# First layer of a two-layer decoder trunk: order of VectorE's work around the first scores, lambdas on GpSimd, shorter root chains, and a later broadcast of the FFN's row roots

## The chip, the cores and the metric

One core of one Trainium2 chip runs the whole program. The metric is device time in microseconds (us) of one execution, the median of 3 runs. The engines are TensorE (PE; PEld is its weight load), VectorE (DVE), ScalarE (ACT), GpSimd (POOL) and SyncE (SP), which issues the loads of the weights. Each engine executes its instructions in program order, and they meet at semaphores.

## The reference, cut to what matters

Two layers work on 256 tokens of width 1024 in float32. Each layer does the following.

```
h = rms_norm(x, norm_mix);  q, k, v = split(h @ w_in)          # 16 heads of 64: 4 diff, 6 dilated, 6 MoBA
q, k = rotary(rms_norm(q)), rotary(rms_norm(k))                # per head (diff: per half head of 32)
lam = exp(sum(lambda_q1 * lambda_k1)) - exp(sum(lambda_q2 * lambda_k2)) + lam_init
diff heads:  p = softmax(q1 k1) - lam * softmax(q2 k2);  o = rms_norm(p v) * (1 - lam_init)
x = x + concat(heads) @ w_out
x = x + memory_cross_attention(rms_norm(x), rms_norm(mem))     # 4 heads, 256 memory rows
x = x + swiglu(rms_norm(x))                                    # d_ff 2816
```

Every rms_norm needs a reciprocal square root of a mean of squares: for x, for the memory rows, and for each head of the queries and keys.

## The kernel before

**Split products.** The matmuls that touch weights are float32 products in three parts. A weight unit of 128 x 2048 values is loaded into `raw`. ACT rounds it to `whi` (`split_hi`), DVE makes the rest `wlo = raw - whi` (`split_lo`, line 927), and PE multiplies (hi, whi), (hi, wlo) and (lo, whi). There are three buffers of each (`RING = 3`). Unit u + 3 is loaded when both splits of unit u are done, and ACT's `split_hi` of unit u + 3 waits until PE has used unit u.

**The grid g.** The first part of each layer (q, k, v, the memory's keys and values, the output projection, and attention woven between them) is laid out by hand on a grid of steps g. At each g PE runs one piece of four matmuls of 512 columns (line 1572). Unit u is used by the six pieces from g = 6u on. Its `whi` is needed at 6u and its `wlo` one piece later. The other steps are placed by constants that name the g at which an engine's loop issues them. All engines walk the same g, each in its own loop, so these constants fix the order on each engine and not the time.

**Around the change, on DVE**, in the order of the loop body for one g: `mem_lo_part`, `mask_max` (masked scores and their maximum, line 1174), `combine` (line 1183 on), `qkT_out` (copies half of the transposed keys, even e, or queries, odd e, out of PSUM, lines 1155 and 1157), `reduce_squares` (line 1081), `lambdas`, `lambda_ends`, the memory rows' root at `MEM_ROOT_AT`, `split_lo`, then `norm_k` with `rope_k` or `norm_q` at `CHAIN_AT`. In the first 60 steps DVE therefore goes: g 7 split of unit 3; 10 `lambdas`; 13 squares 0, split 4; 14 `norm_k(0)`, `rope_k(0)`; 15 `lambda_ends`; 19 memory low part 0, split 5; 20 to 22 memory low parts 1 to 3; 25 squares 1, split 6; 26 `norm_q(0)`; 31 split 7; 32 `qkT_out(0)`; 37 squares 2, split 8; 40 memory root; 43 `qkT_out(1)`, split 9; 45 `mask_max` 0 and 1, `norm_k(1)`, `rope_k(1)`; 47 `mask_max` 2 and 3; 49 `combine` 0 and 1, squares 3, split 10; 53 `norm_q(1)`; 55 `mask_max` 4 and 5, split 11.

**On PE**: `transpose_qk(e)` (line 1665) at g = 32, 43, 58, 72. Even e are keys and wait for DVE's `rope_k`, odd e are queries and wait for GpSimd's `rope_q`. `score(d)` (line 1701) is at g = 45, 47, 55, 61 and waits for the maxima of the pair before (`nmax`), and for d = 0 for both copies of `qkT_out(1)`. The transposes of the probabilities `transpose_p` (line 1713) are at g = 54, 57 and wait for `combine`.

**On GpSimd**: `rope_q(half)` (lines 541 to 544). Its first four instructions wait for the squares of the queries, the other four for `norm_q`'s scaled queries. **On ACT**: the chunks of the projection out of PSUM (line 665), their squares (line 675), `split_hi` (line 605), the exponentials (line 697), and at g = `LAM_AT` + 3 the exponential of the lambdas (line 788), the first Exp of the program.

**Roots.** The heads' roots are computed on DVE by an integer first guess and three Newton steps of three small instructions, each waiting for the one before (`rsqrt`, `minus_rsqrt`, lines 936 to 955). The roots of x's rows and of the memory's rows are asked of GpSimd.

**FFN.** `gate_up(0, 0)` and `gate_up(0, 1)` open the FFN on PE (line 1978). Between them PE waits for `rs_diag` and broadcasts the roots of x's rows with a matmul with ones (line 2006); DVE copies the result to `rs_row` (line 1403). The roots are first used in `gate_step(0, 0)`.

Of the kernel before, what the change touches and what calls it, by code (L numbers as in the profile page):

```python
# [29 lines left out]
P = 128  # L30
F32 = mybir.dt.float32
F32R = mybir.dt.float32r
I32 = mybir.dt.int32
# [5 lines left out]
SEQ = 256  # L39
# [61 lines left out]
def trunk(nc, x, mem, w, gains, consts, out):  # L101
    with ExitStack() as ctx:
        def sb(name, shape, dt=F32):
            return ctx.enter_context(nc.sbuf_tensor(name, shape, dt))

        def signal(name, per_layer=1):
            return Signal(ctx.enter_context(nc.semaphore(name)), per_layer)
# [66 lines left out]
        h_root = sb("h_root", [P, 8])  # L174
        lam_dot = sb("lam_dot", [P, 2, DEPTH])
        lam_exp = sb("lam_exp", [P, 2, DEPTH])
        neg_lam = sb("neg_lam", [P, DEPTH])
# [43 lines left out]
        s_ones = signal("ones_set")  # L221
        s_lam = signal("lambda_ready")
        s_cs = signal("angles_ready")
        s_sin = signal("sines_ready")
# [230 lines left out]
        def _(pool):  # L455
# [53 lines left out]
            def norm_heads(y, gain, ready):  # L509
# [6 lines left out]
                    .then_inc(ready.sem, 1)  # L516

            pool.wait_ge(s_ones.sem, 1)
            for layer in range(DEPTH):
# [9 lines left out]
                ins.then_inc(s_tab.sem, 1)  # L529
                pool.wait_ge(s_tab.sem, s_tab.at(layer, 1))  # L530

                def rope_q(half):
# [378 lines left out]
        def _(dve):  # L911
            links = [0]

            def link(ins):

                links[0] += 1
                ins.then_inc(dve_chain.sem, 1)
                dve.wait_ge(dve_chain.sem, links[0])
# [12 lines left out]

            def rsqrt(n):


                v, h, y, t = (a[:, 0:n] for a in (nv, nh, ny, nt))
                dve.tensor_scalar(h, v, -0.5, None, ALU.mult)
                link(dve.tensor_scalar(y.bitcast(I32), v.bitcast(I32), -0.5, 1597463007.0, ALU.mult, ALU.add))
                for _ in range(3):
                    link(dve.tensor_tensor(t, y, h, ALU.mult))
                    link(dve.tensor_tensor(t, t, y, ALU.mult))  # L940
                    link(dve.scalar_tensor_tensor(y, t, 1.5, y, ALU.add, ALU.mult))

            def minus_rsqrt(n, out):


                v, h, y, t = (a[:, 0:n] for a in (nv, nh, ny, nt))
                dve.tensor_scalar(h, v, 0.5, None, ALU.mult)
                link(dve.tensor_scalar(y.bitcast(I32), v.bitcast(I32), -0.5, 1597463007.0, ALU.mult, ALU.add))
                for step in range(3):
                    link(dve.tensor_tensor(t, y, h, ALU.mult))  # L950
                    link(dve.tensor_tensor(t, t, y, ALU.mult))
                    if step < 2:
                        link(dve.scalar_tensor_tensor(y, t, -1.5, y, ALU.add, ALU.mult))
                    else:
                        link(dve.scalar_tensor_tensor(out, t.rearrange("p (t g) -> p t g", t=T), -1.5,
                                                      y.rearrange("p (t g) -> p t g", t=T), ALU.add, ALU.mult))

            def mean_eps(dst, sums, width):
                link(dve.tensor_scalar(dst, sums, 1.0 / width, EPS, ALU.mult, ALU.add))

# [59 lines left out]
            def lambdas():  # L1020

                dve.wait_ge(s_small.sem, 16)
                for i in range(2):
                    for l in range(DEPTH):
                        link(dve.tensor_tensor_reduce(nt[:, 0:32], lam_in[2 * i][:, l, :], lam_in[2 * i + 1][:, l, :],
                                                      1.0, 0.0, ALU.mult, ALU.add, lam_dot[:, i, l:l + 1]))
                for l in range(DEPTH):
                    ins = dve.tensor_scalar(g_sub[:, l, :], g_sub[:, l, :], 1.0 - lam_init(l), None, ALU.mult)

                    dve.tensor_tensor(g_km[:, l, :], g_km[:, l, :], g_qm[:, l, :], ALU.mult)  # L1030
                ins = dve.memset(nt[:, 0:32], 0.0)
                ins.then_inc(s_lam.sem, 1)

# [12 lines left out]
            for layer in range(DEPTH):  # L1046
# [37 lines left out]
                def norm_q(half):  # L1084

                    dve.wait_ge(reduced.sem, reduced.at(layer, 2 * half + 2))
                    n, first = ((12, 0), (8, 12))[half]
                    v = nv[:, 0:T * n].rearrange("p (t g) -> p t g", t=T)
                    sums = g32[:, 0]
                    if half == 0:  # L1090
                        dve.tensor_scalar(v[:, :, 0:8], sums[:, :, 0:8], 1.0, 32 * EPS, ALU.mult, ALU.add)
                        two = sums[:, :, 8:16].rearrange("p t (g w) -> p t g w", w=2)
                        link(dve.tensor_tensor(v[:, :, 8:12], two[:, :, :, 0], two[:, :, :, 1], ALU.add))
                        mean_eps(v[:, :, 8:12], v[:, :, 8:12], HD)
                    else:
                        dve.tensor_scalar(v[:, :, 0:2], sums[:, :, 0:2], 1.0 / HD, EPS, ALU.mult, ALU.add)
                        link(dve.tensor_scalar(v[:, :, 2:8], sums[:, :, 2:8], 1.0, HD * EPS, ALU.mult, ALU.add))
                    r = q_root[:, :, first:first + n]
                    minus_rsqrt(T * n, r)
                    a, b = ((8, 12), (0, 2))[half]  # L1100
                    z = heads_of_half(0, half)[:, :, ((256, 512), (0, 128))[half][0]:((256, 512), (0, 128))[half][1]]
                    z = z.rearrange("p t (g w) -> p t g w", w=HD)
                    for t in range(T):
                        ins = dve.scalar_tensor_tensor(z[:, t], z[:, t], -1.0,
                                                       r[:, t, a:b].unsqueeze(2).to_broadcast((P, b - a, HD)),
                                                       ALU.mult, ALU.mult)
                    ins.then_inc(scaled.sem, 1)

                def norm_k(half):
# [5 lines left out]
                    if half == 0:  # L1115
                        dve.tensor_scalar(v[:, :, 0:8], sums[:, :, 0:8], 1.0 / 32, EPS, ALU.mult, ALU.add)
# [5 lines left out]
                    rsqrt(T * n)  # L1122
                    r = ny[:, 0:T * n].rearrange("p (t g) -> p t g", t=T)
# [118 lines left out]
                for g in range(6, LAST + 1):  # L1242
# [9 lines left out]
                    for e in range(4):  # L1252
                        if g == QKT_AT[e]:
                            qkT_out(e)
                        if g == 12 * QK_CHUNKS[e] + 13:
                            reduce_squares(e)
# [226 lines left out]
        def _(pe):  # L1483
# [50 lines left out]
            for layer in range(DEPTH):  # L1534
# [114 lines left out]
                def transpose_qk(e):  # L1649
# [288 lines left out]
                output(1, (1,), (1, 2))  # L1938

                def gate_up(pair, b):  # L1940

# [22 lines left out]
                    for part, chunks in steps if b == 0 else ((part, range(KC)) for part in range(3)):  # L1964
# [69 lines left out]

CHAIN_AT = (14, 26, 45, 53)
QKT_AT = (32, 43, 58, 72)
# [61 lines left out]
def last_chunk(pair, b):  # L2098

    return isinstance(pair, int) and pair == PAIRS - 1 and b == 1  # L2100


# [90 lines left out]
```

## Time and profile before

| | us |
|---|---|
| median of 3 runs | 698.07 (697.97 to 698.45) |
| profiled execution | 698.69 |
| its span, first to last instruction | 696.9 |
| outside the span in that execution | 1.8 |
| PE busy in the span | 687.4 (99%) |
| DVE busy | 508.5 (73%) |
| ACT busy | 392.6 (56%) |
| GpSimd busy | 88.3 (13%) |
| granted TensorE clock, mean | 1.000 |

A busy time of PE is modelled from starts that overlap, so it hides waits below about 0.2 us. A line of the timeline reads: start, duration, engine, line, operation, output<-inputs, count, and in brackets the idle time of the engine before it with what ended it.

### The profile page before, as it was taken

The page shows a single profiled execution, that of the slowest core. Times are in us where ns is not written, and L with a number is a line of the kernel's source. Part 1 is how long each engine was busy: PE and PEld are TensorE (multiplying, and loading weights), DVE is VectorE, ACT ScalarE, POOL GpSimd, SP SyncE. Part 2 cuts the span into 40 slices and gives each one's busy share as a digit, 9 for nine tenths or more (in the row PEclk, how much of TensorE's full clock was granted, in tenths as well). Part 3 has the DMA queues.
Part 4 walks back from the last instruction along what each step waited for, and adds up shares of the span by engine and source line. Part 5 has one row for each costly group of instructions (what it writes and reads, how often), then busy time and mean ns, then how long its engine had stood idle before and what let it go on. Part 6 is the DMA issues. An engine that isn't in the chain of part 4 may idle for free.

```text
span 696.9 us, 10774 instructions
## 1 busy us (share of the span) xinstructions
PE 687.4 (99%) x3782; PEld 570.6 (82%) x3782; DVE 508.5 (73%) x1019; ACT 392.6 (56%) x637; POOL 88.3 (13%) x88
## 2 busy tenths in 40 slices
PE   8999999999999999999999999999999999999998
PEld 7876777788888888888888778778898888888886
DVE  5899977586766666666679898775777666666665
ACT  6965776477444444444566658764774444444442
POOL 5130111218000000000032210202530000000000
PEclk9999999999999999999999999999999999999999
DMA  9945341245576656666555635113365666666641
GB/s 325 327 130 178 123 162 57 85 122 156 160 222 187 181 181 181 181 181 184 186 174 199 228 118 179 64 61 112 100 213 141 196 200 197 199 194 194 186 120 61
DMA packets 121249, 115.66 MB, mean 166 GB/s; under 512 B 2688, under 2 KB 95104, under 8 KB 121216
## 3 DMA queue, kind: packets, MB, share of 16 engines
q1 hardware_dynamic: 120640, 114.31, 52.8%
q10 hardware_dynamic: 576, 0.93, 0.4%
q8 instruction: 19, 0.31, 0.2%
q14 instruction: 14, 0.11, 0.0%
HBM read 114.17 MB, written 1.05 MB: 165 GB/s over the span
## 4 chain that ended last, share of the span: by engine, by line
PE 81%; DVE 10%; ACT 3%; POOL 2%; issue 1%; DMA 1%; SPq 0%; ACTq 0%; POOLq 0%; DVEq 0%
PE ps L1951 21%; PE ps L1572 15%; PE ps L1956 11%; PE ps L1997 6%; PE ps L1998 6%; PE ps L1999 6%; DVE wlo L927 3%; PE ps L1643 3%; POOL wlo L497 2%; PE ps L1978 2%; PE ps L1701 2%; PE ps L1519 2%; PE ps L1713 2%; PE ps L1749 1%; DMA raw<-in_w_in 1%
## 5 line engine op out<-in xcount | busy, mean ns | idle before, releaser
L927 DVE TENSOR_TENSOR wlo<-raw,whi 128x2048 fp32r<-128x2048 f32 (+1 forms) x95 | 212.0, 2248 | 41.2 <-ACT whi L605 39.1
L605 ACT ACTIVATE whi<-raw 128x2048 fp32r<-128x2048 f32 (+1 forms) x102 | 188.7, 1876 | 14.7 <-PE ps L1572 8.1
L1951 PE MATMUL ps<-both,whi 128*128 128x512 f32 x640 | 159.2, 391 | 0.0
L1951 PEld LDWEIGHTS ps<-both,whi 128*128 128x128 f32 x640 | 117.7, 188 | 22.7
L1572 PE MATMUL ps<-whi,both 128*128 128x512 f32 x384 | 99.6, 396 | 1.3 <-ACT both L617 0.7
L1956 PEld LDWEIGHTS ps<-both,wlo 128*128 128x128 f32 x640 | 87.4, 191 | 6.2
L865 ACT ACTIVATE qkv<-ps 128x512 f32<-128x512 f32 x42 | 25.2, 599 | 114.3 <-PE ps L1956 113.6
L1956 PE MATMUL ps<-both,wlo 128*128 128x256 f32 x640 | 89.3, 283 | 0.0
L1572 PEld LDWEIGHTS ps<-whi,both 128*128 128x128 f32 x384 | 70.5, 188 | 17.2 <-issue 1.7
L1997 PE MATMUL ps<-whi,ahi 128*128 128x512 f32 x176 | 69.1, 393 | 0.0
L1998 PE MATMUL ps<-wlo,ahi 128*128 128x512 f32 x176 | 69.0, 392 | 0.0
L1999 PE MATMUL ps<-whi,alo 128*128 128x512 f32 x176 | 68.5, 389 | 0.0
L1414 DVE TENSOR_TENSOR qkv<-ps,qkv 128x512 f32<-128x512 f32 x42 | 28.9, 688 | 46.7 <-ACT qkv L865 46.6
L497 POOL TENSOR_TENSOR wlo<-raw,whi 128x2048 fp32r<-128x2048 f32 x7 | 32.0, 4606 | 183.6 <-DVE wlo L1468 179.5
L873 ACT ACTIVATE qkv<-qkv 128x256 f32<-128x256 f32 x44 | 18.4, 418 | 64.5 <-DVE qkv L1419 64.5
L1572 PE MATMUL ps<-wlo,both 128*128 128x512 f32 x192 | 53.4, 401 | 0.0
L697 ACT ACTIVATE sq<-sq,nm 128x128 f32<-128x128 f32 x80 | 35.5, 448 | 19.4 <-DVE nm L1174 19.4
L1572 PEld LDWEIGHTS ps<-wlo,both 128*128 128x128 f32 x192 | 34.6, 188 | 9.4 <-issue 2.7
L617 ACT ACTIVATE both<-ps,starter 128x128 fp32r<-128x128 f32 x96 | 26.6, 378 | 24.8 <-PE ps L1492 24.8
L1999 PEld LDWEIGHTS ps<-whi,alo 128*128 128x128 f32 x176 | 33.1, 188 | 7.2
L1997 PEld LDWEIGHTS ps<-whi,ahi 128*128 128x128 f32 x176 | 33.3, 189 | 5.7
L1998 PEld LDWEIGHTS ps<-wlo,ahi 128*128 128x128 f32 x176 | 33.3, 189 | 5.2
(214 smaller groups left out, 907.8 us busy)
## 6 DMA issues: line engine op xcount, KB each, us to landing
raw<-in_w_gate_up SPq DMA_DIRECT2D x88, 512.0 KB, 5.0
raw<-in_w_in SPq DMA_DIRECT2D x23, 1024.0 KB, 5.2
raw<-in_w_down SPq DMA_DIRECT2D x22, 1024.0 KB, 4.9
raw<-in_w_out SPq DMA_DIRECT2D x8, 1024.0 KB, 5.0
raw<-in_w_mkv SPq DMA_DIRECT2D x4, 1024.0 KB, 5.2
raw<-in_w_mq SPq DMA_DIRECT2D x4, 512.0 KB, 3.5
raw<-in_w_mo SPq DMA_DIRECT2D x2, 1024.0 KB, 4.7
xs<-in_x SPq DMA_DIRECT2D x4, 256.0 KB, 5.8
```

Of the source, the lines that this page charges most:

```text
L497: pool.tensor_tensor(wlo[s][:, 0:n], raw[s][:, 0:n], whi[s][:, 0:n].bitcast(F32), ALU.subtract)\
L605: ins = act.activation(whi[s][:, cols], raw[s][:, cols], ACT.Copy)
L617: ins = act.activation(thi[:, c, tok], ps[:, X_BANKS[b][q], k * P:(k + 1) * P], ACT.Copy, scale=gain)
L697: ins = act.activation(prob[n % 4][:, a:b], prob[n % 4][:, a:b], ACT.Exp, bias=nm[:, n, t:t + 1], scale=-1.0, accum_out=zs[:, n, t:t + 1])
L927: ins = dve.tensor_tensor(wlo[s][:, cols], raw[s][:, cols], hi, ALU.subtract)
L1414: dve.tensor_tensor(gu[b], gu_banks(b, 0), small_gu[b], ALU.add).then_inc(gu_done.sem, 1)
L1572: ins = pe.matmul(ps[:, acc, :], x_part[:, k0 + k, t * P:(t + 1) * P], w_part[s][:, 512 * k:512 * k + 512], start=first and k == 0 and par ...
L1951: pe.matmul(ps[:, bank, :], whi[s][:, a:a + P], both[:, :, k, :], start=(k == 0), stop=False)
L1956: ins = pe.matmul(ps[:, bank, 0:256], wlo[s][:, a:a + P], thi[:, k, :], start=False, stop=(k == KC - 1))
L1997: pe.matmul(acc, ahi[b][:, tok], whi[s][:, a:a + 512], start=first, stop=False)
L1998: pe.matmul(acc, ahi[b][:, tok], wlo[s][:, a:a + 512], start=False, stop=False)
L1999: ins = pe.matmul(acc, alo[b][:, tok], whi[s][:, a:a + 512], start=False, stop=last)
```

## The change

- `norm_k(1)` with `rope_k(1)` moves in the first layer from g = 45 to 50 on DVE (`CHAIN_AT[0][2]`).
- DVE's splits of units 8 and 9 move in the first layer from g = 37 and 43 to 45 and 49 (`LO_AT`).
- DVE's copy of the first half of the keys, `qkT_out(0)`, moves in the first layer from g = 32 to 27, ahead of the split of unit 7. PE's transposes stay at 32.
- The memory rows' root moves from g = 40 to 44.
- `lambdas` moves from g = 10 to 20, `lambda_ends` to 25 and ACT's exponential of them to 23. GpSimd makes the products and scales two gains ahead of its first `rope_q`; DVE keeps one reduction of 128 elements in place of the 13 instructions of before.
- `rsqrt` and `minus_rsqrt` become `cubic_root`: a first guess and two steps of four instructions each, in both layers. It has 9 instructions where 11 stood.
- PE's transposes of the first keys wait for two of the memory's four low parts, and those of the first queries for all four, where the former waited for all four.
- The broadcast of the row roots moves on PE from between the two `gate_up` of the first pair to after the first 16 matmuls of the second.

```diff
+            def lambda_products():
+                pool.wait_ge(s_small.sem, 16)
+                pairs = lam_products[:].rearrange("p (i l n) -> p i l n", i=2, l=DEPTH)
+                pool.tensor_tensor(pairs[:, 0], lam_in[0], lam_in[1], ALU.mult)
+                pool.tensor_tensor(pairs[:, 1], lam_in[2], lam_in[3], ALU.mult).then_inc(s_lam_products.sem, 1)
+                for l in range(DEPTH):
+                    pool.tensor_scalar(g_sub[:, l, :], g_sub[:, l, :], 1.0 - lam_init(l), None, ALU.mult)
+                link(pool.tensor_tensor(g_km, g_km, g_qm, ALU.mult))
...
-            def rsqrt(n):
...
+            def cubic_root(n, sign, out=None):
+                v, y, t, u = (a[:, 0:n] for a in (nv, ny, nt, nh))
+                link(dve.tensor_scalar(y.bitcast(I32), v.bitcast(I32), -0.5, 1597463007.0 - (sign < 0) * 2.0 ** 31,
+                                       ALU.mult, ALU.add))
+                for c in (1.0, ROOT_STEP):
+                    link(dve.tensor_tensor(t, y, v, ALU.mult))
                     link(dve.tensor_tensor(t, t, y, ALU.mult))
+                    link(dve.scalar_tensor_tensor(u, t, -10.0 / 3.0 * c, t, ALU.add, ALU.mult))
+                    if c == 1.0 or out is None:
+                        link(dve.scalar_tensor_tensor(y, u, 5.0 * c * c, y, ALU.add, ALU.mult))
...
             def lambdas():
-                dve.wait_ge(s_small.sem, 16)
...
+                dve.wait_ge(s_lam_products.sem, 1)
+                dve.tensor_reduce(lam_dot[:], lam_products[:].rearrange("p (i l n) -> p i l n", i=2, l=DEPTH), AX_X, ALU.add)\
+                   .then_inc(s_lam.sem, 1)
...
-                        if g == QKT_AT[e]:
+                        if g == QKT_DVE_AT[layer][e]:
                             qkT_out(e)
...
-                    if g % 6 == 1 and g // 6 + 2 < DVE_LO:
-                        split_lo(layer, g // 6 + 2)
+                    for u in range(3, DVE_LO):
+                        if g == LO_AT[layer][u - 3]:
+                            split_lo(layer, u)
                     for e in range(4):
-                        if g == CHAIN_AT[e]:
+                        if g == CHAIN_AT[layer][e]:
...
-                    if layer == e == 0:
-                        pe.wait_ge(m_lo.sem, 4)
+                    if layer == 0 and e < 2:
+                        pe.wait_ge(m_lo.sem, (2, 4)[e])
...
+                        if b and part == 0:
+                            rs_of_tokens()
...
-                pe.wait_ge(diag_ready.sem, diag_ready.at(layer, 1))
-                pe.matmul(ps[:, 4, 0:SEQ], ones[:], rs_diag, start=True, stop=True).then_inc(row_ps.sem, 1)
...
-CHAIN_AT = (14, 26, 45, 53)
+CHAIN_AT = ((14, 26, 50, 53), (14, 26, 45, 53))
+LO_AT = [[6 * (u - 2) + 1 for u in range(3, 18)] for _ in range(2)]
+LO_AT[0][8 - 3], LO_AT[0][9 - 3] = 45, 49
+QKT_DVE_AT = ((27, 43, 58, 72), (32, 43, 58, 72))
...
-LAM_AT = 10
-MEM_ROOT_AT = 40
+LAM_AT = 20
+MEM_ROOT_AT = 44
```

## Rows read from the trace of the kernel before

**Rows 1.** The page: granted TensorE clock in 40 slices of the span, in tenths.

```profile
PEclk9999999999999999999999999999999999999999
```

**Rows 2.** Timeline of PE in the first layer.

```profile
41.64 1.06 PE L1665 MATMUL ps<-starter,qkv 128*128 128x128 f32 x8 [0.70 <-DVE mlo L994]
...
52.57 1.04 PE L1665 MATMUL ps<-starter,qkv 128*128 128x128 f32 x8
...
56.23 0.93 PE L1701 MATMUL ps<-kT,qT 32*128 32x128 f32 x8 [0.80 <-DVE qT L1155]
...
67.59 0.55 PE L1713 MATMUL ps<-starter,sq 128*128 128x128 f32 x3 [0.41 <-DVE sq L1188]
...
73.06 1.03 PE L1665 MATMUL ps<-starter,qkv 128*128 128x128 f32 x8
...
77.13 0.93 PE L1701 MATMUL ps<-kT,qT 32*128 32x128 f32 x8 [0.30 <-DVE nm L1174]
```

**Rows 3.** Chain that ended last, second layer: start, us, what.

```profile
357.94 26.32 PE ps L1572 x116
```

**Rows 4.** Timeline of PE in the second layer.

```profile
407.14 1.07 PE L1572 MATMUL ps<-whi,both 128*128 128x512 f32 x4
408.26 0.55 PE L1713 MATMUL ps<-starter,sq 128*128 128x128 f32 x3
...
415.52 1.98 PE L1572 MATMUL ps<-whi,both 128*128 128x512 f32 x8
417.78 0.93 PE L1701 MATMUL ps<-kT,qT 32*128 32x128 f32 x8 [0.28 <-DVE nm L1174]
```

**Rows 5.** One group of DVE from 36.8 to 77: busy, mean ns, idle before.

```profile
L927 DVE TENSOR_TENSOR wlo<-raw,whi 128x2048 fp32r<-128x2048 f32 x7 | 16.1, 2304 | 0.4 <-ACT whi L605 0.4
```

**Rows 6.** Timeline of DVE in the first layer.

```profile
31.27 0.18 DVE L939 TENSOR_TENSOR nt<-ny,nh 128x24 f32<-128x24 f32 x1
...
33.23 0.69 DVE L1127 TENSOR_TENSOR qkv<-qkv,ny 128x512 f32<-128x512 f32 x1
...
36.37 0.15 DVE L1037 TENSOR_TENSOR neg_lam<-lam_exp 128x2 f32<-128x2 f32 x1
...
48.15 2.29 DVE L927 TENSOR_TENSOR wlo<-raw,whi 128x2048 fp32r<-128x2048 f32 x1
...
59.55 0.17 DVE L959 TENSOR_SCALAR nv<-g 128x16 f32<-128x16 f32 x1
...
64.99 0.34 DVE L1174 CUSTOM_DVE_ANT_0 sq<-ps,table,q_root 128x128 f32<-128x128 f32 x1
...
72.79 0.16 DVE L1096 TENSOR_SCALAR nv<-g 128x4 f32<-128x4 f32 x1
...
76.99 2.29 DVE L927 TENSOR_TENSOR wlo<-raw,whi 128x2048 fp32r<-128x2048 f32 x1
```

**Rows 7.** Timeline of ACT: second chunk's squares, and the Silu table in the FFN.

```profile
36.79 1.07 ACT L675 ACTIVATE sqc<-qkv 128x1024 f32<-128x1024 f32 x1
...
175.48 1.28 ACT L873 ACT_TABLE_LOAD   x1
178.85 0.42 ACT L873 ACTIVATE qkv<-qkv 128x256 f32<-128x256 f32 x1 [2.09 <-DVE qkv L1419]
```

**Rows 8.** Timeline of GpSimd: second half of the first `rope_q`.

```profile
48.38 2.38 POOL L541 TENSOR_TENSOR rope_pool<-qkv,tab 128x128 f32<-128x128 f32 x1 [7.26 <-DVE qkv L1104]
...
51.53 0.32 POOL L544 TENSOR_TENSOR qkv<-rope_pool 128x64 f32<-128x64 f32 x1
```

**Rows 9.** Timelines at the opening of the FFN: PE, then DVE, then PE.

```profile
173.59 1.12 PE L1978 MATMUL ps<-both,whi 128*128 128x256 f32 x8
174.92 0.70 PE L2006 MATMUL ps<-qkv,ones 128*128 128x256 f32 x2 [0.21 <-DVE qkv L1399]
...
180.09 0.42 DVE L1440 TENSOR_TENSOR alo<-qkv,ahi 128x256 fp32r<-128x256 f32 x1
...
181.21 0.40 PE L1997 MATMUL ps<-whi,ahi 128*128 128x512 f32 x1
```

More of the change, by code:

```diff
@@ L175, in trunk @@
         lam_dot = sb("lam_dot", [P, 2, DEPTH])
+        lam_products = sb("lam_products", [P, 2 * DEPTH * 32])
         lam_exp = sb("lam_exp", [P, 2, DEPTH])
@@ L222, in trunk @@
         s_lam = signal("lambda_ready")
+        s_lam_products = signal("lambda_products")
         s_cs = signal("angles_ready")
@@ L530, in _ @@
                 pool.wait_ge(s_tab.sem, s_tab.at(layer, 1))
+                if layer == 0:
+                    lambda_products()
                 def rope_q(half):
@@ L930, in split_lo @@
                 ins.then_inc(lo_done[s].sem, 1)
-            def rsqrt(n):
[L935 to L939, printed above, removed]
-                    link(dve.tensor_tensor(t, t, y, ALU.mult))
-                    link(dve.scalar_tensor_tensor(y, t, 1.5, y, ALU.add, ALU.mult))
@@ L943, in minus_rsqrt @@
[L943 to L953, printed above, removed]
+            def cubic_root(n, sign, out=None):
[4 more added lines that the diff above has]
+                    link(dve.tensor_tensor(t, y, v, ALU.mult))
+                    link(dve.tensor_tensor(t, t, y, ALU.mult))
+                    link(dve.scalar_tensor_tensor(u, t, -10.0 / 3.0 * c, t, ALU.add, ALU.mult))
+                    if c == 1.0 or out is None:
+                        link(dve.scalar_tensor_tensor(y, u, 5.0 * c * c, y, ALU.add, ALU.mult))
@@ L954, in minus_rsqrt @@
                     else:
-                        link(dve.scalar_tensor_tensor(out, t.rearrange("p (t g) -> p t g", t=T), -1.5,
+                        link(dve.scalar_tensor_tensor(out, u.rearrange("p (t g) -> p t g", t=T), 5.0 * c * c,
                                                       y.rearrange("p (t g) -> p t g", t=T), ALU.add, ALU.mult))
             def mean_eps(dst, sums, width):
-                link(dve.tensor_scalar(dst, sums, 1.0 / width, EPS, ALU.mult, ALU.add))
+                link(dve.tensor_scalar(dst, sums, ROOT_SCALE / width, ROOT_SCALE * EPS, ALU.mult, ALU.add))
@@ L1020, in lambdas @@
             def lambdas():
-                dve.wait_ge(s_small.sem, 16)
[L1023 to L1032, printed above, removed]
+                dve.wait_ge(s_lam_products.sem, 1)
+                dve.tensor_reduce(lam_dot[:], lam_products[:].rearrange("p (i l n) -> p i l n", i=2, l=DEPTH), AX_X, ALU.add)\
+                   .then_inc(s_lam.sem, 1)
             def lambda_ends():
@@ L1090, in norm_q @@
                     if half == 0:
-                        dve.tensor_scalar(v[:, :, 0:8], sums[:, :, 0:8], 1.0, 32 * EPS, ALU.mult, ALU.add)
+                        dve.tensor_scalar(v[:, :, 0:8], sums[:, :, 0:8], ROOT_SCALE, ROOT_SCALE * 32 * EPS, ALU.mult, ALU.add)
                         two = sums[:, :, 8:16].rearrange("p t (g w) -> p t g w", w=2)
@@ L1095, in norm_q @@
                     else:
-                        dve.tensor_scalar(v[:, :, 0:2], sums[:, :, 0:2], 1.0 / HD, EPS, ALU.mult, ALU.add)
-                        link(dve.tensor_scalar(v[:, :, 2:8], sums[:, :, 2:8], 1.0, HD * EPS, ALU.mult, ALU.add))
+                        dve.tensor_scalar(v[:, :, 0:2], sums[:, :, 0:2], ROOT_SCALE / HD, ROOT_SCALE * EPS, ALU.mult, ALU.add)
+                        link(dve.tensor_scalar(v[:, :, 2:8], sums[:, :, 2:8], ROOT_SCALE, ROOT_SCALE * HD * EPS, ALU.mult, ALU.add))
                     r = q_root[:, :, first:first + n]
-                    minus_rsqrt(T * n, r)
+                    cubic_root(T * n, -1, r)
                     a, b = ((8, 12), (0, 2))[half]
@@ L1115, in norm_k @@
                     if half == 0:
-                        dve.tensor_scalar(v[:, :, 0:8], sums[:, :, 0:8], 1.0 / 32, EPS, ALU.mult, ALU.add)
+                        dve.tensor_scalar(v[:, :, 0:8], sums[:, :, 0:8], ROOT_SCALE / 32, ROOT_SCALE * EPS, ALU.mult, ALU.add)
                         two = sums[:, :, 8:16].rearrange("p t (g w) -> p t g w", w=2)
@@ L1121, in norm_k @@
                         mean_eps(v, sums[:, :, 0:8], HD)
-                    rsqrt(T * n)
+                    cubic_root(T * n, 1)
                     r = ny[:, 0:T * n].rearrange("p (t g) -> p t g", t=T)
@@ L1938, in _, with rs_of_tokens @@
                 output(1, (1,), (1, 2))
+                def rs_of_tokens():
+                    pe.wait_ge(diag_ready.sem, diag_ready.at(layer, 1))
+                    pe.matmul(ps[:, 4, 0:SEQ], ones[:], rs_diag, start=True, stop=True).then_inc(row_ps.sem, 1)
                 def gate_up(pair, b):
@@ L2100, in last_chunk @@
     return isinstance(pair, int) and pair == PAIRS - 1 and b == 1
+ROOT_STEP = 64.0 / 9.0
+ROOT_SCALE = ROOT_STEP ** 6
 def lam_init(layer):
```

## The prediction, made blind

> **What bounds the kernel now.** I read the chain that ended last first. It is PE nearly throughout, except for the stretch from 18 to 77 us in the first layer, where links of DVE lie between PE's. The bracketed waits of PE's timeline say where: 0.70 at the first keys' transposes for the memory's low parts, 0.80 at the first scores for the copy of the queries, 0.41 at g = 54 for `combine`, 0.30 at g = 61 for the maxima [rows 2]. With about 0.5 between the first two scores, that is some 2.7 us. Apart from the opening of the span and one wait in each FFN [rows 9], PE shows nothing else of that size. The second layer runs the same grid, and PE keeps there a pace of 26.32 / 116 = 0.227 us a matmul, 0.91 a piece [rows 3]. Its small waits at g = 54 and 61 are seen by that pace: 407.14 + 0.92 = 408.06 against 408.26, and 415.52 + 1.92 = 417.44 against 417.78 [rows 4], 0.2 and 0.34. From g = 61 on, the layers lie the same distance apart at every piece (417.78 - 77.13 = 340.65 [rows 2, 4]). So what the change is worth in the first layer is the time at which the scores of g = 61 start, 77.13 now. All that follows is shifted by that.
>
> **The roots, both layers.** The nine linked instructions of a root take 33.23 - 31.27 = 1.96 us, 0.22 each [rows 6], with two more ahead of them, the first of which costs 0.1. Now there are one and eight, so a root is shorter by 0.22 + 0.09 = 0.3. Each layer has four. *Second layer:* the roots at g = 14 and 26 are hidden, for PE runs at pace there. The third is in front of `combine`, which comes 0.3 earlier and ends the 0.2 of g = 54. With the fourth the maxima of g = 61 come 0.6 earlier, more than 0.34, so PE goes on at pace there too. Gain 0.2 + 0.34 = 0.54, bounds 0.3 and 0.6. The queue behind DVE (its splits) comes earlier alike.
>
> **The broadcast in the FFN.** PE's eight matmuls from 173.59 would end their issue at about 174.55, and the broadcast starts at 174.92 [rows 9]: 0.36 lost. Behind 16 more matmuls (1.9 us) it starts at 176.5, well after the diagonal is ready. Its result comes at about 177.2, when DVE ends the split that it does in between, so `rs_row` isn't later. The cover is thin further on too: `alo` is done at 180.09 + 0.42 = 180.51, and PE then wants it at 181.21 - 0.36 = 180.85 [rows 9]. Gain 0.36 in each layer, 0.7 in all, bounds 0.3 and 0.8.
>
> **The first layer, by work alone.** DVE is the bound from the memory's low parts to g = 61, with 0.4 us of idle before the split of unit 10 [rows 5] and 0.1 before the second `combine`. Both orders hold the same work up to the maxima of g = 61, which ends at 76.99 [rows 6]. Off go four roots, 1.2, and these idle times, 0.5. On comes the reduction of the lambdas, 0.25 (bounds 0.15 and 0.4; small linked steps take 0.22, the squares of eight times the size more). The four products and the scalings that went to GpSimd save nothing: they lay in a gap in which DVE would have waited for the first squares. So DVE alone would be done at 75.5, and PE would gain 1.6. The wait of 0.70 for the memory's low parts goes, but PE then waits at the next transposes instead, as follows.
>
> **The first layer, by the new order.** I walked the four queues forward with the durations of the rows. New waits on DVE come in this order.
> - *Lambdas.* `rope_k(0)` ends at 36.37 - 0.3 = 36.1 [rows 6]. A low part, split 5, another low part and the reduction bring `lambda_ready` at 39.75. ACT comes to the exponential long before, at about 35, and is in order: behind it stand the chunk out of PSUM and the squares of the queries, which started at 36.79 [rows 7]. They now start at 40.6 and end at 41.7. DVE wants them at 40.9. Then `whi` of unit 6 follows, at 43.5, and split 6 waits for it a little more: 0.8 + 0.25 = 1.05. The table of Exp costs nothing extra, if it is loaded ahead of the wait as Silu's is (loaded at 175.48, used at 178.85 after a wait [rows 7]).
> - *First queries.* `norm_q(0)` ends at N = 48.85 (48.15 now [rows 6]). GpSimd's rotation then ran from 48.38 to 51.85, since its first instruction took 2.38 and ended only after DVE's split of 48.15 to 50.44 [rows 6, 8]. The last came 3.7 behind N. Now DVE's copy of the keys, 0.65, stands between N and split 7, so the blocking split ends 0.65 later, and the queries come at N + 4.35 = 53.2 at the worst. If the first instruction slips through in that gap, it is 52.75. PE, which would be there at 51.65 (52.57 now [rows 2], less 0.9 by the wait that went), stands until 52.8 to 53.25. The transposes' second half takes 1.1. DVE has the copy, split 7 and a reduction to do, 4.0, and waits 1.1 to 1.55 for it.
> - *First scores.* They start 2.75 after these transposes and are read 0.95 later, at 56.5 to 57.0. DVE is through with the copy and the memory root at 55.5 to 56.0, and waits 1.0. Splits 8 and 9, which filled this time before, are now behind.
> - *Second `combine`*, for the exponentials: 0.3.
>
> Sum of new waits 3.45 to 3.9, so the maxima of g = 61 come at 75.5 + 3.7 = 79.2, less 0.2 because the splits now run beside fewer instructions of GpSimd: 79.0. That is 2.0 later than 76.99, with bounds of 0.4 (GpSimd never blocked) and 2.4.
>
> **What PE sees.** It starts the first scores at about 55.8 and is ahead of now until g = 54 (some 65.9 against 67.59). It would reach the keys' transposes of g = 58 at 65.9 + 5.5 = 71.4. But `rope_k(1)` is no longer done at 64.99 [rows 6], eight us early. It now stands behind splits 8, 9 and 10, both `combine` and a reduction, and ends before `norm_q(1)` and the maxima, that is 4.2 - 0.3 = 3.9 before 79.0 [rows 6]: at 75.1. PE waits 3.7 us in one piece there, starts at 75.2 (73.06 now), needs 3.75 to g = 61 and starts those scores at 79.1. So the stall isn't removed but gathered in one place. `norm_k(1)` itself is 64.99 - 59.55 = 5.4 long [rows 6], one reason why it can't be late.
>
> **A rule beside it.** The row shows that a GpSimd instruction started in a split ends after it. The Trainium skill, GPSIMD Engine Reference, section 1 (Specifications), says that GpSimd shares its SBUF interfaces with VectorE where the latter has two SBUF inputs or a 2-port mode. By that rule the key copy, which reads PSUM, blocks nothing and the split does, so the better case of 52.75 would hold and the result would be 0.4 less than by the worst. The trace agrees as far as it goes.
>
> **Sum.** First layer +2.0, second layer -0.54, FFN -0.7: +0.75 of the profiled execution's 698.69 (span 696.9 and 1.8 outside it). I put the same difference on the median of the three runs, 698.07, which lies 0.6 below that execution: 698.8. Two tenths of a per cent are 1.4 us, about what can be told from no change.
>
> **The rivals.**
> - *No blocking.* GpSimd gets through before split 7; the queries are 1.6 earlier, the first layer ends at +0.4: 697.2. Against it: every rotation instruction that overlaps a split in the trace is long.
> - *DVE's bare work* (faster). The waits that I placed between engines don't arise or are filled, because the copies of keys and queries now come ahead of two low parts. Then g = 61 is at 75.5 and the first layer gains 1.6: 695.2. It decides where the new waits of DVE sum to less than about 1.5. For it: DVE is the only bound of the stretch now. Against it: the queue positions above.
> - *The clock falls* (slower). PE stands 3.7 us at g = 58, longer than anything in the trace of before, whose granted clock is full in all 40 slices [rows 1]. At the lower level (1.2 of 2.4 GHz) a piece would take 1.8 in place of 0.91. If it stays there for as long as the wait was, half of 3.7 is lost: 700.6. It decides at a wait of a length that no row shows. The Trainium skill, TensorE: Matmul & The Clock Gate, "Why this matters for your kernels", advises against gaps above about 3 us between bursts; by it this rival would hold.
> - *The table after the wait* (slower). If Exp's table is loaded only after `lambda_ready`, its 1.28 [rows 7] stands on ACT's way to the squares: 700.0. Against it: Silu's row.
>
> **How the numbers follow.** Forecast 0.52, no blocking 0.13, bare work 0.18, clock 0.11, table 0.06. Faster: bare work and a little of no blocking, 0.20. Slower: clock, table and the upper end of the forecast, 0.22. Same: 0.58. The range goes from halfway to the bare work, 696.2, to just past the table's time, 700.3; outside are the core of the bare work and most of the clock's case.
>
> **What would show it.** In the profile after: ACT idle before the exponential of the lambdas, some 3.5 to 4 us; DVE idle before its reduction of the queries' squares, before the queries' copy and before the first maxima; PE with one long wait at the transposes of g = 58 released by `rope_k`, and g = 61 at 79. In the second layer the scores of g = 61 0.5 us closer to the layer's start, and no wait at line 2006. I am wrong if PE's wait at g = 58 is under 2 us, if its clock row falls, or if `rope_k(1)` ends before 73.

## The result, and the profile after the change

The changed kernel takes 700.70 us (median of 6 runs, 700.40 to 701.76), the kernel before, run beside it, 698.19 (6 runs, 697.97 to 698.45). The ratio is 1.0038 [1.0028, 1.0048]: slower by 2.5 us, with the whole interval beyond 0.2%. I had forecast 698.8 and a range up to 700.3, so the time lies outside the range, on the side of the rival that I had given 0.11, the clock that falls.

The mean granted clock was 0.998 in four of the six runs (700.40 to 700.79 us) and 0.994 in the other two (701.48 and 701.76); before the change it was 1.000 in the profiled execution.

The profiled execution took 700.4 us (span 698.6), against 698.69 (696.9) before. These two differ by 1.7, not by the 2.5 of the medians: the profiled execution of before lies 0.5 above its kernel's median, and that of the changed kernel is the fastest of its six. The page shows no sign of the clock: its slices of 17 us still read 9 everywhere, as in [rows 1]. Only the mean over the span, which was 1.000, has moved:

```profile
core 0: 698.6 us, clock 0.998
```

PE's timeline in the first layer, which answers to [rows 2] (start, us, what, in brackets the wait before it):

```profile
52.54 1.09 PE L1662 MATMUL ps<-starter,qkv 128*128 128x128 f32 x8 [1.13 <-POOL qkv L558]
...
65.68 0.49 PE L1710 MATMUL ps<-starter,sq 128*128 128x128 f32 x3
...
70.08 1.17 PE L1569 MATMUL ps<-whi,both 128*128 128x512 f32 x4
75.20 1.97 PE L1662 MATMUL ps<-starter,qkv 128*128 128x128 f32 x8 [3.95 <-DVE qkv L1138]
76.82 1.82 PE L1569 MATMUL ps<-wlo,both 128*128 128x512 f32 x4
78.47 2.02 PE L1569 MATMUL ps<-whi,both 128*128 128x512 f32 x8
80.42 0.92 PE L1698 MATMUL ps<-kT,qT 32*128 32x128 f32 x8
```

Up to 75.20 this is the walk of the prediction: PE ahead of before until g = 54 (65.68; I said 65.9), then one wait for `rope_k(1)` of 3.95 (3.7) that ends at 75.20 (75.2). What comes next isn't. Eight transposes that took 1.03 before take 1.97, and four weight matmuls 1.82. The scores of g = 61 start at 80.42, not at 79.1.

A table of windows over the same stretch tells why (columns: window, its length, busy time of PE, PEld, DVE, ACT and POOL with instructions in parentheses, granted clock of PE, DMA share, GB/s):

```profile
70.00:75.00 5.00, 1.25 (x7) 0.73 (x5) 4.45 (x19) 0.00 (x0) 0.04 (x1) 0.98 0.95 359
75.00:76.00 1.00, 0.80 (x4) 0.80 (x5) 0.86 (x7) 0.00 (x0) 0.00 (x0) 0.50 0.06 25
...
77.00:78.00 1.00, 1.00 (x4) 0.81 (x4) 0.95 (x6) 0.00 (x0) 0.14 (x1) 0.50 0.00 0
78.00:79.00 1.00, 1.00 (x6) 0.77 (x5) 1.00 (x7) 0.58 (x3) 0.92 (x4) 0.88 0.00 0
79.00:80.00 1.00, 1.00 (x6) 0.83 (x5) 1.00 (x3) 1.00 (x4) 0.00 (x0) 1.00 0.02 8
```

At the end of PE's long wait the granted clock drops to 0.50, the lower of its two levels (1.2 of 2.4 GHz), and it is back after 78. In the trace it is low from 74.82 to 78.24, 3.4 us. PE had done nothing for some 3.6 us when it fell, and did work at half speed for the 3 us after 75.20.

DVE's timeline, which answers to [rows 6]:

```profile
41.36 1.22 DVE L1077 TENSOR_REDUCE g<-sqc 128x32 f32<-128x1024 f32 x1 [0.75 <-ACT sqc L689]
...
43.24 2.29 DVE L941 TENSOR_TENSOR wlo<-raw,whi 128x2048 fp32r<-128x2048 f32 x1 [0.22 <-ACT whi L619]
...
53.67 0.69 DVE L1151 COPY qT<-ps 128x512 f32<-128x512 f32 x1 [1.04 <-PE ps L1662]
...
56.38 0.35 DVE L1170 CUSTOM_DVE_ANT_0 sq<-ps,table,q_root 128x128 f32<-128x128 f32 x1 [0.93 <-PE ps L1698]
...
65.12 4.68 DVE L941 TENSOR_TENSOR wlo<-raw,whi 128x2048 fp32r<-128x2048 f32 x2
...
74.89 0.25 DVE L1138 TENSOR_TENSOR qkv<-rope_dve 128x96 f32<-128x96 f32 x1
...
78.98 2.29 DVE L941 TENSOR_TENSOR wlo<-raw,whi 128x2048 fp32r<-128x2048 f32 x1
```

The four new waits of DVE are there: 0.75 + 0.22 for the first queries' squares, 1.04 before the queries' copy, 0.93 before the first maxima. The splits of 65.12 (units 9 and 10) stand ahead of `norm_k(1)` and `rope_k(1)`, whose last instruction, at 74.89, is the one that PE waits for. The maxima of g = 61 end where the next split starts, at 78.98 (79.0 said, 76.99 before).

ACT waits in front of the exponential of the lambdas, with its table loaded ahead of the wait, and the queries' squares are behind it, 3.5 us later than in [rows 7]:

```profile
34.45 1.28 ACT L802 ACT_TABLE_LOAD   x1
39.45 0.20 ACT L802 ACTIVATE lam_exp<-lam_dot 128x4 f32<-128x4 f32 x1 [3.72 <-DVE lam_dot L1027]
39.56 0.67 ACT L679 ACTIVATE qkv<-ps,rs 128x512 f32<-128x512 f32 x1
40.27 1.06 ACT L689 ACTIVATE sqc<-qkv 128x1024 f32<-128x1024 f32 x1
```

On GpSimd, where [rows 8] show 2.38 for the first instruction of the rotation, that one now slips through and the second is the long one:

```profile
48.78 0.46 POOL L555 TENSOR_TENSOR rope_pool<-qkv,tab 128x128 f32<-128x128 f32 x1 [5.75 <-DVE qkv L1100]
49.20 2.60 POOL L556 TENSOR_TENSOR rope_pool<-qkv,tab 128x128 f32<-128x128 f32 x1
```

DVE's split 7 starts at 49.22. So this was the better of my two cases: PE's transposes start at 52.54, against the 52.8 to 53.25 that I had walked.

Then PE in the FFN and in the second layer, which answers to [rows 9] and [rows 4]:

```profile
176.86 3.04 PE L1980 MATMUL ps<-both,whi 128*128 128x256 f32 x24
179.74 0.59 PE L1940 MATMUL ps<-qkv,ones 128*128 128x256 f32 x2
179.98 2.26 PE L1980 MATMUL ps<-both,wlo 128*128 128x256 f32 x16
...
183.99 0.40 PE L2001 MATMUL ps<-whi,ahi 128*128 128x512 f32 x1
...
419.97 0.93 PE L1698 MATMUL ps<-kT,qT 32*128 32x128 f32 x8
```

The broadcast (179.74) has no wait, nor have the second layer's scores. By these anchors the span's +1.7 splits up as follows:

| Stretch (PE start to PE start) | before | after | difference | forecast |
|---|---|---|---|---|
| to the memory rows' first transposes | 27.01 | 26.69 | -0.3 | 0 |
| from there to the scores of g = 61, layer 1 | 50.12 | 53.73 | +3.6 | +2.0 |
| to the FFN's first down matmul | 104.08 | 103.57 | -0.5 | -0.36 |
| to the scores of g = 61, layer 2 | 236.57 | 235.98 | -0.6 | -0.54 |
| to the second FFN's first down matmul | 104.08 | 103.54 | -0.5 | -0.36 |

All terms but one are within about 0.3. The -0.3 of the first row is no gain that can be told: in the ten traces of this case those transposes start anywhere from 26.38 to 27.02. The first layer has 1.6 more than forecast. Its maxima end 2.0 later while the whole stretch began 0.3 earlier, so DVE's order costs 2.3; the other 1.3 is between `rope_k(1)` and g = 61, at the low clock.

### The profile page after: what moved, and what is told of

Read it like the earlier page. It is cut to its first block, busy times and chain, and to the rows that moved or that the text cites. A ratio compares the mean times of both kernels' runs of the same rounds, so it can differ in the third digit from the quotient of the medians.

```text
span 698.6 us, 10753 instructions
## 1 busy us (share of the span) xinstructions
PE 688.4 (99%) x3782; PEld 572.1 (82%) x3782; DVE 505.3 (72%) x991; ACT 392.2 (56%) x637; POOL 94.3 (14%) x93
## 3 DMA queue, kind: packets, MB, share of 16 engines
HBM read 114.17 MB, written 1.05 MB: 165 GB/s over the span
## 4 chain that ended last, share of the span: by engine, by line
PE 92%; DVE 5%; ACT 1%; DMA 1%; issue 1%; POOL 1%; SPq 0%; DVEq 0%; ACTq 0%; POOLq 0%
PE ps L1569 21%; PE ps L1953 21%; PE ps L1958 11%; PE ps L2001 6%; PE ps L2002 6%; PE ps L2003 6%; PE ps L1980 3%; PE ps L1640 3%; PE ps L1698 2%; PE ps L1516 2%; DVE wlo L941 2%; PE ps L1710 2%; PE ps L1885 2%; PE ps L1489 1%; PE ps L1746 1%; PE ps L1858 1%
```

## The experiments

Every kernel ran beside the kernel before on the same chip (one chip for e1 to e4, another for e5 to e8): beside e1 to e4 the kernel before had 698.24 in the median of 30 runs, beside e5 to e8 698.27 in 27, with a clock of 0.999 or 1.000. These two values of the mean are called the full clock below; 0.998 and less are called low. Three questions stood against each other: is the second half of the loss the clock; is it one long wait that lowers it; and does the loss that is left come from the queue of DVE, or from the parts (roots, lambdas, broadcast)?

| Kernel | median, us | runs | lowest to highest | ratio [95%] | PE's waits, 49 to 82 us |
|---|---|---|---|---|---|
| after | 700.70 | 6 | 700.40 to 701.76 | 1.0038 [1.0028, 1.0048] | 1.13, 3.95 |
| e1 | 700.88 | 7 | 699.07 to 702.03 | 1.0031 [1.0020, 1.0042] | 1.1, 1.69, 2.27 |
| e2 | 699.20 | 11 | 698.78 to 699.54 | 1.0013 [1.0004, 1.0022] | 1.1, filled + 1.23 |
| e3 | 699.54 | 11 | 698.77 to 700.53 | 1.0018 [1.0009, 1.0027] | 3.94 |
| e4 | 697.44 | 11 | 696.77 to 699.10 | 0.9991 [0.9982, 1.0000] | 0.91, 1.42, 0.48 |
| e5 | 698.39 | 11 | 697.84 to 700.48 | 1.0002 [0.9993, 1.0011] | 0.88, 1.42 |
| e6 | 697.33 | 11 | 695.42 to 698.90 | 0.9986 [0.9976, 0.9995] | 1.98 |
| e7 | 697.02 | 11 | 696.50 to 697.25 | 0.9980 [0.9971, 0.9989] | 0.5, 0.5 |
| e8 | 695.51 | 5 | 695.44 to 695.78 | 0.9960 [0.9947, 0.9974] | 1.22 |

### e2: the long wait filled

DVE's order is left as the change has it. PE is given matmuls of ones, into the bank of the transposes that follow, to do in its wait.

```diff
@@ PE, at every g @@
+                    if layer == 0 and g == QKT_AT[2]:
+                        warm_up(FILL, QKT_BANKS[2][0])
+FILL = 12
```

> The changed kernel with 12 more transposes-sized products of ones (24 matmuls of 128 columns, some 3.6 us at full clock) on PE right before the transposes of g = 58 in the first layer, into the bank that these overwrite. They add no work that the output needs. Clock theory: PE's idle time there falls from 3.95 to about 0.4 us, the clock stays 1.000, the eight transposes take 1.0 in place of 1.97 us, the scores of g = 61 start at 79.1, the time is 698.9 us. Rival (the loss stands in DVE's queue only): nothing changes, 700.5 us, or more by the added matmuls.

PE's timeline, and one window:

```profile
71.01 2.84 PE L1526 MATMUL ps<-ones 128*128 128x128 f32 x24
75.09 1.10 PE L1662 MATMUL ps<-starter,qkv 128*128 128x128 f32 x8 [1.23 <-DVE qkv L1138]
...
79.01 0.92 PE L1698 MATMUL ps<-kT,qT 32*128 32x128 f32 x8
```

```profile
75.00:76.00 1.00, 0.91 (x9) 0.92 (x9) 0.86 (x7) 0.00 (x0) 0.00 (x0) 1.00 0.12 47
```

The filling took 2.84 us and not the 3.6 that I expected, so 1.23 us of the wait stays empty. The keys come no sooner (75.09), but the clock stays at 1.00 in the window behind the wait, the transposes take 1.10, and g = 61 starts at 79.01, where I had put it. From the transposes to g = 61 it is 3.92 here and 5.22 in the changed kernel: 1.3 for the clock. The medians say 1.50 (700.70 - 699.20), in which the changed kernel's two runs at 0.994 have a part: its four at 0.998 have a median of 700.58, 1.38 above e2. What is left by the medians, +0.96 over before, stands against the prediction's +0.75; by the two profiled spans (697.3 and 696.9) it is +0.4. So the clock is about 1.5 of the 2.5, and the forecast without it lies between these two.

### e1: one split behind the keys

```diff
 LO_AT[0][8 - 3], LO_AT[0][9 - 3] = 45, 49
+LO_AT[0][10 - 3] = 51
```

> The changed kernel with one more constant: DVE's split of unit 10 in the first layer goes from g = 49 to 51, behind norm_k(1) and rope_k(1). DVE's work and its sum stay the same, so the maxima of g = 61 still end near 79.0. Clock theory (the long wait lets TensorE's clock fall, and that is what came on top of the forecast): the keys are ready 2.2 us earlier, PE's wait at the transposes of g = 58 is 1.7 us in place of 3.95, the granted clock stays 1.000, the scores of g = 61 start at 79.1 in place of 80.4, and the time is 698.9 us or less. Rival (DVE's late end alone, or a transposition that is slow for another reason, makes the loss): 700.5 us, as the changed kernel.

PE's timeline, and one window:

```profile
72.65 1.09 PE L1662 MATMUL ps<-starter,qkv 128*128 128x128 f32 x8 [1.69 <-DVE qkv L1138]
...
78.76 1.49 PE L1698 MATMUL ps<-kT,qT 32*128 32x128 f32 x8 [2.27 <-DVE nm L1170]
```

```profile
79.00:80.00 1.00, 1.00 (x8) 0.52 (x6) 1.00 (x1) 1.00 (x4) 0.00 (x0) 0.50 0.18 66
```

This was a miss, and the miss taught most. The keys were 2.5 earlier, and the maxima of g = 61 as late as in the changed kernel, both as I had said; what I had overlooked is that PE, which comes to g = 61 earlier, must then wait there for these maxima. The wait was split in two, 1.69 and 2.27, neither as long as the one of 3.95. Still the clock fell, at 78.97, and stayed low for 6.83 us, twice as long as after the single wait; the profiled run took 702.03. Of the seven runs, the two whose mean clock was 0.999 and 1.000 took 699.32 and 699.07, about e2's time; the other five (0.995 to 0.998) 700.68 to 702.03. At the full clock, then, keys that come 2.5 earlier gain nothing, since DVE's maxima set g = 61. A single long wait isn't what decides about the clock, and the time of a kernel depends on whether the clock falls in that very execution.

### e3: the lambdas' exponential late

```diff
-                    if layer == 0 and g == LAM_AT + 3:
+                    if layer == 0 and g == LAM_EXP_AT:
-                    if layer == 0 and g == LAM_AT + 5:
+                    if layer == 0 and g == LAM_ENDS_AT:
+LAM_EXP_AT, LAM_ENDS_AT = 31, 44
```

> The changed kernel with ACT's exponential of the lambdas at g = 31 in place of 23 and DVE's lambda_ends at g = 44 in place of 25. Theory of the queues: ACT no longer stands 3.7 us before the exponential, the squares of the queries come 1.6 us earlier, DVE loses its waits of 0.75 and 0.22 us before the squares' reduction and split 6, and the maxima of g = 61 end 1.0 to 1.2 us earlier. PE's wait at g = 58 stays 3.7 to 4 us long, because PE comes earlier too, and the clock still falls: 699.4 us. Rival (ACT's wait is hidden by other slack): 700.5 us.

ACT's timeline, then PE's:

```profile
35.58 1.06 ACT L689 ACTIVATE sqc<-qkv 128x1024 f32<-128x1024 f32 x1
...
42.28 0.20 ACT L802 ACTIVATE lam_exp<-lam_dot 128x4 f32<-128x4 f32 x1
```

```profile
74.08 1.14 PE L1662 MATMUL ps<-starter,qkv 128*128 128x128 f32 x8 [3.94 <-DVE qkv L1138]
...
79.45 0.92 PE L1698 MATMUL ps<-kT,qT 32*128 32x128 f32 x8
```

With the exponential at g = 31 the squares are back at 35.58, and everything of DVE comes about 1 us earlier, as expected. PE's wait keeps its length, for PE is earlier too, and so does the loss of clock (0.994 to 0.998 in the runs). The median, 699.54 against 699.4 expected, is 1.16 below the changed kernel: that is what ACT, blocked in order, costs.

### e4 and e5: the old order, with the new parts

e4 takes DVE's old positions back, and keeps the roots, GpSimd's lambdas and the moved broadcast. e5 takes the broadcast back too.

```diff
-CHAIN_AT = ((14, 26, 50, 53), (14, 26, 45, 53))
+CHAIN_AT = ((14, 26, 45, 53), (14, 26, 45, 53))
-LO_AT[0][8 - 3], LO_AT[0][9 - 3] = 45, 49
-QKT_DVE_AT = ((27, 43, 58, 72), (32, 43, 58, 72))
+QKT_DVE_AT = ((32, 43, 58, 72), (32, 43, 58, 72))
-MEM_ROOT_AT = 44
+MEM_ROOT_AT = 40
@@ only e5: PE, between the gate_ups of the FFN @@
-                        if b and part == 0:
-                            rs_of_tokens()
+                rs_of_tokens()
```

> The changed kernel with the first layer's order of DVE as before (norm_k(1) at 45, splits 8 and 9 at 37 and 43, the keys' copy at 32, memory root at 40). Left of the change: roots of 9 instructions, lambdas on GpSimd at g = 20, the two low-part waits, the late broadcast. Theory: the order alone makes the loss. PE has no wait above 1.5 us in the first layer, clock 1.000, scores of g = 61 at 77.1 as before (what the roots save there is lost again to ACT's wait for the lambdas), second layer -0.55, FFN -1.0: 696.6 us. Rival (the lambdas or the roots cost more than they save): 698 us or more.

> The changed kernel with the first layer's order of DVE as before, and the broadcast of the row roots back between the two gate_up of the first pair. Left: the roots, the lambdas on GpSimd, the low-part waits. Theory: the late broadcast is worth 0.5 us in each layer, as the two traces show, so this kernel takes 1.0 us more than the one with the old order alone (697.4): 698.4 us. Rival (what the broadcast gains is given back before the next layer): 697.4 us.

In e4 the keys of g = 58 are in time again, and PE waits elsewhere (timeline):

```profile
52.53 1.09 PE L1662 MATMUL ps<-starter,qkv 128*128 128x128 f32 x8 [0.91 <-POOL qkv L558]
...
56.89 0.92 PE L1698 MATMUL ps<-kT,qT 32*128 32x128 f32 x8 [1.42 <-DVE qT L1151]
...
77.19 0.92 PE L1698 MATMUL ps<-kT,qT 32*128 32x128 f32 x8
```

g = 61 starts at 77.19, as before the change (77.13): roots and lambdas together gain the first layer nothing. The roots alone gain it 1.1 (e7, below). In e4 ACT still stands 3.39 us before the exponential of the lambdas, and DVE behind it 0.75 and 0.23, which e7 has not, so the lambdas take back most of what the roots give. e4 is 3.26 faster than the changed kernel, so the moved positions of DVE, with the clock that they cost, are the whole loss. I had expected 696.6 and a full clock; it is 0.8 more, and the clock was low in six of the 11 runs. The five at the full clock have a median of 697.12, so 0.5 of the miss isn't the clock. e5 came as expected (698.39 against 698.4), and the broadcast's new place is worth 697.44 against 698.39: 0.95, or 0.48 a layer, which agrees with the 0.5 a layer of the table above. The runs at the full clock alone say the same: 697.12 against 698.08, five of each.

Both kernels lose clock in six of 11 runs. e5's profiled run (700.48) was one, and its windows and timeline show it after waits of only 0.88 and 1.42 us, with work in between:

```profile
55.00:59.00 4.00, 2.58 (x16) 1.68 (x15) 3.15 (x6) 0.69 (x1) 0.73 (x1) 1.00 0.78 256
60.00:65.00 5.00, 5.00 (x17) 3.21 (x16) 4.49 (x19) 2.28 (x9) 0.00 (x0) 0.50 0.57 210
```

```profile
60.56 1.65 PE L1698 MATMUL ps<-kT,qT 32*128 32x128 f32 x8
```

### e7: the roots alone

The kernel before, with `cubic_root` for both roots (and the scaling it needs) and nothing else.

```diff
-            def rsqrt(n):
-            def minus_rsqrt(n, out):
+            def cubic_root(n, sign, out=None):
...
-                    minus_rsqrt(T * n, r)
+                    cubic_root(T * n, -1, r)
-                    rsqrt(T * n)
+                    cubic_root(T * n, 1)
```

> The kernel before with the roots of two steps alone, in both layers. Theory: DVE is the only bound up to the scores of g = 61 in the first layer, so three of the four roots (0.3 us each) move them by 0.9 to 1.2 us, and the second layer gains 0.55 by its two small waits: 696.6 us. Rival (the stretch is bound by PE or by ACT as well): 0.55 us, 697.7.

PE's timeline:

```profile
76.04 0.92 PE L1691 MATMUL ps<-kT,qT 32*128 32x128 f32 x8
```

This part, alone, is a gain: 697.02, 1.25 less than before, with g = 61 at 76.04 (77.13 in [rows 2]) and the clock full in all 11 runs. I had expected 696.6, so it came 0.4 short, though well clear of the rival's 697.7. In the traces the terms are there: g = 61 is 1.09 earlier (0.2 of which lies ahead of the memory rows' first transposes, where the traces differ anyway), and the second layer 0.58 shorter. The old order in the first layer could use the shorter roots.

### e6 and e8: another order

Both move the lambdas' end as e3 does, leave the keys' copy at g = 32, and put `rope_k(1)` ahead of a split again; e8 differs from e6 by one number, the place of split 10.

```diff
-CHAIN_AT = ((14, 26, 50, 53), (14, 26, 45, 53))
+CHAIN_AT = ((14, 26, 49, 53), (14, 26, 45, 53))
-LO_AT[0][8 - 3], LO_AT[0][9 - 3] = 45, 49
+LO_AT[0][9 - 3], LO_AT[0][10 - 3] = 45, 51
-QKT_DVE_AT = ((27, 43, 58, 72), (32, 43, 58, 72))
+QKT_DVE_AT = ((32, 43, 58, 72), (32, 43, 58, 72))
+LAM_EXP_AT, LAM_ENDS_AT = 31, 44
@@ only e8 @@
-LO_AT[0][9 - 3], LO_AT[0][10 - 3] = 45, 51
+LO_AT[0][9 - 3], LO_AT[0][10 - 3] = 45, 55
```

> The changed kernel with another order in the first layer, found by the same walk along the queues: ACT's exponential of the lambdas at g = 31, lambda_ends at 44, the keys' copy at 32, split 8 at 37, split 9 at 45, norm_k(1) and rope_k(1) at 49, split 10 at 51. Theory: DVE always has a split in hand while GpSimd, PE and ACT work on the queries, the keys of g = 58 are ready before PE comes, no wait of PE in the first layer is above 0.5 us, the clock stays 1.000, the scores of g = 61 start at 75.5 (77.1 before), and with 1.6 from the second layer and the FFN the time is 695.4 us. Rival (the walk leaves out a wait that the old order hid): 697 us or more.

> The kernel e6 with split 10 of the first layer at g = 55, behind the maxima of g = 61. Theory: the scores of g = 61 could start at 73.6, but the piece of g = 61 needs split 10, which ends at 75.6, so a wait of 1.2 us moves from the scores to that piece, and the gain over e6 is 0.8 us at most: 694.8 us. Rival (DVE's whole work decides, wherever the split stands): as e6.

e6, PE's timeline and two windows:

```profile
75.66 0.92 PE L1698 MATMUL ps<-kT,qT 32*128 32x128 f32 x8 [1.98 <-DVE nm L1170]
...
77.67 3.44 PE L1569 MATMUL ps<-whi,both 128*128 128x512 f32 x8
```

```profile
77.00:78.00 1.00, 1.00 (x5) 0.82 (x4) 1.00 (x2) 1.00 (x5) 0.00 (x0) 0.69 0.00 0
78.00:79.00 1.00, 1.00 (x4) 0.71 (x4) 0.93 (x4) 1.00 (x4) 0.00 (x0) 0.50 0.17 14
```

The scores of g = 61 start at 75.66, where I had walked them, but PE waits 1.98 there, which I had not seen, and the clock falls afterwards: its mean of 0.69 between 77 and 78 puts the fall at about 77.4, 1.7 us after PE had gone back to work. Eight matmuls take 3.44 in place of 1.98. The clock was low in 9 of 11 runs; the two with a clock of 0.999 took 695.42 and 695.66, the time that I had forecast for all of them.

In e8 split 10 gives way to the maxima (PE's timeline):

```profile
73.61 0.92 PE L1698 MATMUL ps<-kT,qT 32*128 32x128 f32 x8
75.76 1.19 PE L1569 MATMUL ps<-wlo,both 128*128 128x512 f32 x4 [1.22 <-DVE wlo L941]
```

PE now has no wait at g = 61, which starts 3.5 earlier than before the change, and pays 1.22 behind it, where it wants the split that was put off. The clock was full in all five runs. The median, 695.51, is 2.8 below the kernel before and 5.2 below the changed one. It isn't the 694.8 that I expected. e6's two runs at the full clock took 695.42 and 695.66, so at the full clock the two orders are equal as far as five runs and two can tell, which is what the rival said: DVE's whole work decides, wherever split 10 stands. DVE's copy behind that work (line 1153) starts at 77.72 in e6 and 77.82 in e8. What e8 gains over e6's median, 1.8, is the clock. The parts of the change are therefore worth having; its positions were not.

## Why the prediction was right or wrong

- **The reading of what bounds** held: PE's end follows the start of g = 61, which DVE sets in the first layer, and the second layer and the FFN moved as units.
- **The queue walk** was right in its waits, and its end was closer than its parts. Predicted and measured: ACT idle before the exponential 3.5 to 4, 3.72; DVE's waits 1.05, 0.97 (squares and split 6), 1.1 to 1.55, 1.04 (queries), 1.0, 0.93 (scores), 0.3, 0.38 (second `combine`); end of the maxima 79.0, 78.98. It cost 2.3 with the earlier start, 2.0 said; e2 confirms it at +0.96 in all (medians) against +0.75. That 78.98 meets 79.0 is in part luck. The waits sum to 3.3, less than the 3.45 to 3.9 of the walk, and the stretch began 0.3 earlier. With DVE's bare work at 75.5, as I had it, this gives 75.5 + 3.3 - 0.3 = 78.5, so the work between the waits was about 0.5 longer than I had summed; where, stays open. The 0.2 that I took off, for splits that run beside fewer instructions of GpSimd, no run shows. The splits of this stretch took 2.28 or 2.29 both before and after, but for one of 2.43 before and one of 2.48 after.
- **GpSimd behind a split:** the better case held. The instruction that started before split 7 took 0.46, the one that started with it 2.60. The Trainium skill (GPSIMD Engine Reference, section 1, Specifications) says that GpSimd shares its SBUF interfaces with VectorE and that they contend when VectorE's instruction has two SBUF inputs. Both numbers agree with it.
- **Roots in the second layer:** -0.54 said, -0.59 found (e7: -0.58). **Broadcast:** undersized, 0.36 a layer said, 0.5 found (e5: 0.48). I had counted only the gap ahead of the broadcast; it also takes less room itself, 0.24 to the next piece (179.74 to 179.98) where it took 0.35 before (174.92 to 175.27).
- **The table after the wait** and **bare work** are refuted: the load is at 34.45, five us ahead of its use, and the waits of DVE sum to 3.3, far above the 1.5 from which bare work decided.
- **The step that failed** is in "What PE sees": "starts at 75.2 ..., needs 3.75 to g = 61". It needed 5.22, since the clock was at its lower level for the first 3.0 us of it and every matmul cost double there. The forecast put this term at nothing. I had named it as a rival and given it 0.11, arguing that no row shows the length from which it decides. But no row showed that a wait of 3.7 is safe either: the longest of before was 0.8 [rows 2]. So 0.11 had no ground in the rows, and I should have said so. My price for it (half of 3.7, 1.85) was near: 1.3 in the trace, 1.5 by the medians, 2.3 to 2.6 in the two runs at 0.994. The lower end of my range had a slip too: halfway from 698.8 to the bare work's 695.2 is 697.0, not 696.2. It decided nothing.
- **The rival's own wording was wrong too.** "It decides at a wait of a length" isn't what the runs show. The mean clock was low in every run with a wait of 3.95 or 3.94 (6 of after, 11 of e3), in 9 of 11 with one of 1.98 (e6), in 5 of 7 with 1.69 and 2.27 a few us apart (e1), and in 12 of 22 with 0.9, 1.4 and 0.5 (e4, e5). It was never low with waits up to 0.8 (before, e7), in e2's 11 runs with 1.1 and 1.23, or in e8's five with 1.22. Only the profiled runs show where it fell; of the others the mean alone is known. The advice of the Trainium skill (TensorE: Matmul & The Clock Gate, "Why this matters for your kernels") against gaps above about 3 us pointed the right way for the change, but it would have called e6 and e5 safe; the measurement decides. What exactly makes it fall, and why in one execution and not the next, stays open. That idle time of PE is the cause in the changed kernel, and not something else of the new order, is shown by e2 alone, where only the filling differs.

## What to carry to other kernels

When positions in a queue are moved, list for every step that is now behind others when it ended and who wants it: `rope_k(1)` went from eight us early to four late, because split 10, the second pair's maxima, both `combine` and a reduction now stand in front of it, and splits 8 and 9 come later than they did. Small waits at many places that are gathered in one may cost more than their sum: here PE came back from a wait of 3.95 us to half its clock. Take from the trace the longest wait at which the clock stayed full, and treat anything longer as open. Compare variants at the same clock, too: e8 beats e6 by 1.8 in the medians and by nothing in the runs at the full clock. A short spell of low clock doesn't show in a profile's coarse slices: look at the mean clock in its third decimal, at windows of 1 us behind the waits, and at the spread of the runs (before: 1.0 us in 30 runs; e6: 3.5 in 11).

## What the runs showed of the hardware

- The low clock came in spells of 3.4 us (the changed kernel) or twice that, 6.8 us (e1 and e5). A short one cost 1.3 us in the changed kernel (5.22 against e2's 3.92) and about 1.8 in e6 (695.5 in its two runs at the full clock, 697.3 in the median of its seven at 0.997 or 0.998).
- It need not fall in the wait: in e6 it fell some 1.7 us after PE had resumed, in e5 2.0 us after (56.97, and a mean of 0.51 from 59 to 60), and in e1 0.2 us after.
- Matmuls of ones, 24 instructions in 2.84 us, were enough to hold it over a wait of about 4 us in all 11 runs of e2, although 1.23 us of that wait stayed empty.
- A GpSimd operation of 0.46 us took 2.60 when it started together with a DVE split of 2.3 us, and 0.46 when it started 0.4 us ahead of one. Behind the changed kernel's two splits that run back to back (65.12, 4.68 us), two GpSimd operations that take 0.39 elsewhere took 2.47 and 2.43.
